# A second FFN whose up products read a scaled and shifted input from the seventh pair on, and wide down products in both mixers

## Chip, cores and metric

One core of a Trainium2 chip runs the whole program in one launch. The metric is the device time of one execution in microseconds (us).

## What is computed

Two transformer blocks after one another, for 256 tokens of width 1024, everything in float32 (x, c, the weights and the result). The first block, cut to what matters:

```
def modulate(x, w, shift, scale):
    return rms_norm(x, w) * (1 + scale[:, None, :]) + shift[:, None, :]

def swiglu(h, w13, w2):
    gu = jnp.einsum('bsd,df->bsf', h, w13)
    g, u = jnp.split(gu, 2, axis=-1)
    return jnp.einsum('bsf,fd->bsd', jax.nn.silu(g) * u, w2)
...
    mod = (c_act @ w_ada + b_ada).reshape(b, 3, 3, D_MODEL)
    x = x + 0.5 * mod[:, 0, 2] * swiglu(modulate(x, norm_w[0], mod[:, 0, 0], mod[:, 0, 1]), ffn_w13[0], ffn_w2[0])
    x = x + mod[:, 1, 2] * hybrid_mixer(modulate(x, norm_w[1], mod[:, 1, 0], mod[:, 1, 1]), ...)
    x = x + 0.5 * mod[:, 2, 2] * swiglu(modulate(x, norm_w[2], mod[:, 2, 0], mod[:, 2, 1]), ffn_w13[1], ffn_w2[1])
```

The FFN width is 2816 (22 blocks of 128). The second block has a mixer of two attentions with gates and an output product, an FFN of width 4096 with squared relu, and a gated embedding; then a last norm.

## The kernel before

**Split products.** Each float32 operand is split into two fp32r parts, a high one that ScalarE writes and a low one that VectorE makes by subtracting the high part. A product is hi x hi + hi x lo + lo x hi. x lies with features on partitions (`m.x[:, k, :]`, k = 0..7, 256 tokens). A *tile* is one 128 x 128 block of weights against all tokens. `tile` (L516) makes it with three matmuls of 256 columns (258 where two shift columns ride along). `wide_tile` (L521) makes it with two: the high weights against both parts of the tokens at once (512 columns, the second 256 of them into the other half of the bank), then the low weights against the high part (256 columns). Whoever reads the bank then has to add its halves.

**Weights.** They come in units of 16 tiles (128 x 2048 float32, 1 MB) through a raw ring of four slots, loaded by SP (`load`, L1384); the load of a unit waits until the unit four before it has been split. ScalarE writes the high half of a unit in two instructions (`hi`), VectorE the low half in two (`lo`, L2474), into a split ring of four slots. Among the units are *modulation pairs* (`ada`): VectorE multiplies a raw unit by silu(c) and sums it, two columns of `mod` each. The planner (`Plan`) writes the order of all engines in one list: `need` takes units three ahead of TensorE, `fill` and `went` put the pending low halves and modulation steps between the other steps. Each engine executes its steps in this order.

**The second FFN** (`second_ffn`, L1004). Pair j (0 to 21) is one unit: the gate block j and the up block j, 8 k each, into two banks. The input `m.h` is x times a column of gains, without the token factor and the shift, so that TensorE can start before the norm is known; the shift rides along as columns 256 and 257, and `glu_evac2` (L646) multiplies each bank by the row of token factors `rbc` on VectorE (gate_scaled, up_scaled), takes the shift column out with ScalarE (shifts), applies the silu (gate_silu), multiplies (glu2) and splits the product (hid_hi, hid_lo). The norm of the stage, from x_norm at pair 0 to norm_rows at pair 1, gives `rbc`. After pair 4, `load_tables` brings the tables of the second block's mixer and `axial_tables` works on them, after pair 8 `bias_table` and `bias_store` follow. The temporary buffers `tmp` (six of 128 x 512) are not used in this stage.

**Down products** run over f = 0..7, with the banks' sums added to x by `residual` (L2619), followed by the input of the next stage (`hx_hi`, `hx_lo`) and its squares. In the FFNs f < 6 is wide (`wide`, L133), in the mixers (`down_1`, `down_2`) every tile has three matmuls.

## Time and profile before

| | |
|---|---|
| median of 3 runs | 1012.15 us (1011.41 to 1012.33) |
| the profiled execution, its own time | 1011.21 us |
| its span in the profile | 1009.4 us |
| PE (matmuls) busy | 982.6 us, 97% |
| PEld (weight loads) busy | 917.6 us, 91% |
| DVE (VectorE) busy | 774.3 us, 77% |
| ACT (ScalarE) busy | 535.0 us, 53% |
| DMA, mean | 212 GB/s |
| up products of the second FFN | 380.5 to 509.8 us of the span |

Times in views are microseconds from the span's start; ns are marked. "idle before <-X" tells what ended the time in which an engine had nothing to do. Weight loads (PEld) overlap matmuls. In a timeline a row merges instructions of one form that follow each other; "[1.37 <-ACT sb_zb L192]" is idle time before the row and what ended it.

### The profile page before, as it was taken

What the parts mean: (1) busy time and instruction counts of PE and PEld (TensorE: products, weight loads), DVE (VectorE), ACT (ScalarE), POOL (GpSimd) and SP (SyncE); (2) the same over time, 40 slices, a digit from 0 to 9 for tenths busy, and PEclk for the clock granted to TensorE, in tenths of its full rate; (3) what the DMA queues carried; (4) which work ended last, traced back from release to release, by engine and by line L of the source; (5) the groups of instructions that cost most, each with busy time, mean ns of one, the idle gap of its engine ahead of it and who ended that gap; (6) DMA issues with size and microseconds to landing.
All of it is one profiled execution on the core that took longest, in us unless ns stands there. A gap on an engine that the chain in (4) does not pass through costs nothing.

```text
span 1009.4 us, 17305 instructions
## 1 busy us (share of the span) xinstructions
PE 982.6 (97%) x7016; PEld 917.6 (91%) x7016; DVE 774.3 (77%) x1420; ACT 535.0 (53%) x927; POOL 11.8 (1%) x32
## 2 busy tenths in 40 slices
PE   5999999999899999999999999999999999999996
PEld 4999998998898999999998988789999988988895
DVE  6999999879976787685776588556778776677665
ACT  5454554437566555353655545664555555455453
POOL 0000000004000000000000000000000000000000
PEclk9999999999999999999999999999999999999998
DMA  9997999865572664678665535364445555545431
GB/s 336 351 344 272 344 343 340 303 212 210 200 253 99 218 213 181 219 239 224 244 227 184 192 126 209 125 183 136 157 173 178 188 188 189 208 168 181 174 106 42
DMA packets 33677, 213.92 MB, mean 212 GB/s; under 512 B 3773, under 2 KB 6717, under 8 KB 8894
## 3 DMA queue, kind: packets, MB, share of 16 engines
q1 hardware_dynamic: 33310, 211.78, 59.5%
q8 instruction: 55, 0.90, 0.3%
q10 hardware_dynamic: 288, 1.05, 0.3%
q14 instruction: 24, 0.20, 0.1%
HBM read 210.19 MB, written 2.62 MB: 211 GB/s over the span
## 4 chain that ended last, share of the span: by engine, by line
PE 80%; DVE 9%; ACT 4%; DMA 4%; issue 2%; SPq 0%; DVEq 0%; ACTq 0%
PE bank L216 78%; DMA sb_raw<-wts 3%; DVE sb_ring L195 2%; ACT sb_ring L192 2%; PE bank L219 2%; ACT sb_tmp L192 1%; DVE sb_junk L204 1%; DVE sb_tq L195 1%; DVE sb_tmp L195 1%; DMA R<-rows 1%; DVE sb_tmp L201 1%; ACT R L192 0%; DMA sb_x<-xt 0%; DVE R_512r L195 0%; DVE sb_tmp L198 0%
## 5 line engine op out<-in xcount | busy, mean ns | idle before, releaser
L216 PE MATMUL bank<-sb_h,sb_ring 128*128 128x258 f32 (+2 forms) x3776 | 496.0, 292 | 4.1 <-DVE sb_h L201 3.9
L216 PEld LDWEIGHTS bank<-sb_h,sb_ring 128*128 128x128 f32 x3776 | 475.5, 190 | 17.8 <-issue 5.9
L195 DVE TENSOR_TENSOR sb_ring<-sb_raw,sb_ring 128x1024 fp32r<-128x1024 f32 (+1 forms) x324 | 385.6, 1205 | 10.4 <-ACT sb_ring L192 10.3
L192 ACT ACTIVATE sb_ring<-sb_raw 128x1024 fp32r<-128x1024 f32 (+1 forms) x324 | 320.4, 1037 | 80.3 <-DMA sb_raw<-wts 47.5
L216 PE MATMUL bank<-R_512r,sb_ring 128*128 128x256 f32 (+1 forms) x1608 | 225.7, 301 | 0.0
L216 PEld LDWEIGHTS bank<-R_512r,sb_ring 128*128 128x128 f32 x1608 | 211.4, 188 | 12.0 <-issue 0.5
L216 PE MATMUL bank<-sb_ring,sb_h 128*128 128x512 f32 (+1 forms) x504 | 112.5, 378 | 0.0
L216 PEld LDWEIGHTS bank<-sb_ring,sb_h 128*128 128x128 f32 x504 | 87.4, 188 | 16.6
L204 DVE CUSTOM_DVE_ANT_0 sb_junk<-sb_raw,sb_csil,sb_cols 128x1024 bf16<-128x1024 f32 x72 | 92.3, 1282 | 1.8
L216 PE MATMUL bank<-R_1024r,sb_ring 128*128 128x512 f32 (+1 forms) x576 | 91.6, 320 | 0.0
L216 PEld LDWEIGHTS bank<-R_1024r,sb_ring 128*128 128x128 f32 x576 | 82.0, 188 | 8.2
L195 DVE TENSOR_TENSOR sb_tq<-bank,sb_rbc 128x256 f32<-128x256 f32 x87 | 33.9, 420 | 50.8 <-ACT sb_zb L192 25.5
L192 ACT ACTIVATE R_512r<-sb_tq 128x256 fp32r<-128x256 f32 x60 | 25.1, 418 | 76.5 <-DVE sb_tq L195 49.7
L192 ACT ACTIVATE sb_tmp<-bank 128x256 f32<-128x256 f32 (+2 forms) x62 | 27.9, 462 | 30.4 <-PE bank L216 27.8
L192 ACT ACTIVATE sb_tmp<-sb_tmp,sb_smx 128x256 f32<-128x256 f32 (+2 forms) x40 | 20.9, 524 | 35.5 <-DVE sb_smx L204 25.3
L201 DVE SCALAR_TENSOR_TENSOR sb_x<-bank,sb_gcol,sb_x 128x256 f32<-128x256 f32 x36 | 17.4, 482 | 27.8 <-PE bank L216 27.4
L192 ACT ACTIVATE sb_h<-sb_x,sb_cols 128x256 fp32r<-128x256 f32 x24 | 14.2, 591 | 37.5 <-DVE sb_x L201 24.0
L195 DVE TENSOR_TENSOR R_512r<-sb_tq,R_512r 128x256 fp32r<-128x256 f32 x60 | 25.2, 420 | 3.9 <-ACT R_512r L192 3.9
L192 ACT ACTIVATE sb_tq<-bank 128x256 f32<-128x256 f32 (+1 forms) x35 | 12.8, 366 | 27.0 <-PE bank L216 27.0
L195 DVE TENSOR_TENSOR sb_tmp<-bank,sb_tmp 128x256 f32<-128x256 f32 x32 | 12.4, 425 | 19.1 <-ACT sb_tmp L192 19.1
L192 ACT ACTIVATE sb_tq<-sb_tq,sb_zb 128x256 f32<-128x256 f32 x26 | 13.3, 510 | 24.3 <-DVE sb_tq L195 24.1
L219 PE MATMUL bank<-sb_con,sb_tmp 128*128 128x128 f32 (+1 forms) x134 | 21.1, 275 | 2.5 <-ACT sb_tmp L192 1.9
(158 smaller groups left out, 555.8 us busy)
## 6 DMA issues: line engine op xcount, KB each, us to landing
...
```

The lines of the kernel that those rows point to most:

```text
L192: return Issued(self.e and self.e.activation(o, i, func, **kw))
L195: return Issued(self.e and self.e.tensor_tensor(*a))
L201: return Issued(self.e and self.e.scalar_tensor_tensor(*a))
L204: return Issued(self.e and self.e.tensor_tensor_reduce(*a))
L216: return Issued(self.e and self.e.matmul(o, w, m, start=start, stop=stop, skip_group_check=True))
L219: return Issued(self.e and self.e.transpose(o, i, ident))
```

## The change

- `second_ffn` has a second way for pairs 6 to 21. The input, scaled by gain and token factor and shifted (the true `modulate`), is made once into eight tiles with a high and a low part (`scaled_tile`: xr_2 on VectorE, scaled_hi on ScalarE, scaled_lo on VectorE). Tiles 0 and 1 come after the evacuation of pair 2, 2 and 3 after pair 3, 4 and 5 after pair 4, 6 and 7 after pair 5. The first six lie in `tmp`, the last two in the region of the tables' one-hot rows, behind `bias_table`.
- Pairs 6 to 21 are products with `wide_tile` (`up_scaled_2`), and `glu_evac_scaled` adds the halves of the banks: up_half (ScalarE copies the second half), up_added (VectorE), silu_added, glu_added, then hid_hi and hid_lo as before.
- `load_tables` moves from pair 4 to after pair 0, `axial_tables` to after pair 2, `bias_table` and `bias_store` from pair 8 to after pair 3.
- In `down_1` and `down_2` the tiles of f < 6 are wide; `residual` and `residual_2` add the second half of the bank in an instruction of their own, and the one that adds the first half waits for it.

```diff
+SCALED_FROM = 6
...
+    def scaled_tile(self, k, b):
+
+        t = self.m.tq.take()
+        self.add("xr_2", k, t)
+        self.fill()
+        self.add("scaled_hi", k, t, b)
+        self.add("scaled_lo", k, t, b)
+        done(t, ("scaled", k))
+
+    def glu_evac_scaled(self, j, banks):
+
+        s, q = self.m.tq.take(), self.m.tq.take()
+        for i, a in enumerate((s, q)):
+            self.add("up_half", j, i, banks[i], a)
+        for i, a in enumerate((s, q)):
+            self.add("up_added", j, i, banks[i], a)
+            done(banks[i], ("up_added", j, i))
+        self.add("silu_added", j, s)
+        self.fill()
+        self.add("glu_added", j, s, q)
+        done(s, ("glu", "f2", j))
+        self.add("hid_hi", "f2", j, q)
+        self.fill()
+        self.add("hid_lo", "f2", j, q)
+        done(q, ("hid", "f2", j))
...
         first = self.glu2("f2", bk, 0, begin)
-        for j in range(1, NH1):
+        self.add("load_tables")
+        scaled = []
+        for j in range(1, SCALED_FROM):
             banks = self.glu2("f2", bk, j, finish if j == 1 else None)
             if j == 1:
                 self.glu_evac2("f2", first, 0)
             self.glu_evac2("f2", banks, j)
-            if j == 4:
-                self.add("load_tables")
+            for k in range(2 * (j - SCALED_FROM + 4), 2 * (j - SCALED_FROM + 5)):
+                if k >= 0:
+                    scaled.append(m.tmp.take() if k < 6 else None)
+                    self.scaled_tile(k, scaled[k])
+            if j == 2:
                 self.add("axial_tables")
-            if j == 8:
+            if j == 3:
                 b = m.banks[7].take()
                 self.add("bias_table", b)
                 done(b, ("bias_table",))
                 self.add("bias_store")
+        for j in range(SCALED_FROM, NH1):
+            banks = [bk.take(), bk.take()]
+            for k in range(8):
+                for i, b in enumerate(banks):
+                    self.mm(128, "up_scaled_2", j, k, i, b, scaled[k])
+            self.glu_evac_scaled(j, banks)
...
+    def up_scaled_2(self, j, k, i, bank, x):
+        e = self.e
+        if k == 0:
+            self.turn(bank)
+        e.wait_ge(*self.at("scaled", k))
+        self.wide_tile(bank.ap, self.m.scaled(k, x), k == 0, k == 7, *([("up", "f2", j)] if k == 7 and i == 1 else []))
...
+    def xr_2(self, k, t):
+        m, e = self.m, self.e
+        self.turn(t)
+        e.wait_ge(*self.at("rbc", "f2"))
+        e.scalar_tensor_tensor(t.ap, m.x[:, k, :], m.acol[:, 16 + k:17 + k], m.rbc, ALU.mult, ALU.mult).then_inc(
+            *self.up("xr", ("xr_2", k)))
+
+    def scaled_lo(self, k, t, b):
+        m, e = self.m, self.e
+        hi, lo = (m.scaled(k, b)[:, i, :] for i in range(2))
+        e.wait_ge(*self.at("scaled_hi", k))
+        e.scalar_tensor_tensor(lo, t.ap, m.mod[:, 48 + k:49 + k], hi.bitcast(F32), ALU.add, ALU.subtract).then_inc(
+            *self.up("scaled_lo", ("scaled", k)))
...
-        if wide(f) and st != "m1":
+        if wide(f):
```

How the instructions stand now, at three places. In these rows of VectorE `sb_ring<-sb_raw` is a low weight half, `ISA sb_junk,sb_mod` with `ISA sb_mod` a modulation step, `sb_tq<-sb_x,sb_acol,sb_rbc` xr_2 and `parts` a scaled tile's low part.

VectorE, before the change, from hid_lo of pair 2 to hid_lo of pair 3:

```order
L195 TENSOR_TENSOR R_512r<-sb_tq,R_512r 128x256
L204 ISA sb_junk,sb_mod<-sb_raw,sb_csil,sb_cols 128x1024
L204 ISA sb_mod 128x1
L204 ISA sb_junk,sb_mod<-sb_raw,sb_csil,sb_cols 128x1024
L204 ISA sb_mod 128x1
L195 TENSOR_TENSOR sb_tq<-bank,sb_rbc 128x256 x2
L195 TENSOR_TENSOR sb_ring<-sb_raw,sb_ring 128x1024
L201 SCALAR_TENSOR_TENSOR sb_tq<-sb_tq,sb_zb 128x256
L195 TENSOR_TENSOR sb_ring<-sb_raw,sb_ring 128x1024
L195 TENSOR_TENSOR R_512r<-sb_tq,R_512r 128x256
```

VectorE, with the change, from hid_lo of pair 2 to the first step of pair 3's evacuation:

```order
L197 TENSOR_TENSOR R_512r<-sb_tq,R_512r 128x256
L203 SCALAR_TENSOR_TENSOR sb_tq<-sb_x,sb_acol,sb_rbc 128x256
L203 SCALAR_TENSOR_TENSOR parts_50<-sb_tq,sb_mod,parts_50 128x256
L203 SCALAR_TENSOR_TENSOR sb_tq<-sb_x,sb_acol,sb_rbc 128x256
L203 SCALAR_TENSOR_TENSOR parts_51<-sb_tq,sb_mod,parts_51 128x256
L200 TENSOR_SCALAR sb_bhalf<-sb_cols 128x16
L197 TENSOR_TENSOR R_256_144<-R_256_57,R_256_59 128x256
L197 TENSOR_TENSOR R_256_145<-R_256_58,R_256_59 128x4x32 x2
L197 TENSOR_TENSOR R_256_146<-R_256_57,R_256_59 128x256
L197 TENSOR_TENSOR R_256_147<-R_256_58,R_256_59 128x4x32 x2
L206 ISA sb_junk,sb_mod<-sb_raw,sb_csil,sb_cols 128x1024
```

Two scaled tiles and the axial tables, which stood behind pair 4, are now ahead of the modulation pair and of pair 3's evacuation.

VectorE, with the change, from the second weight half in pair 5's evacuation to the modulation pair that comes before pair 6's evacuation; the two tiles here are the last that pair 6 reads:

```order
L197 TENSOR_TENSOR sb_ring<-sb_raw,sb_ring 128x1024
L197 TENSOR_TENSOR R_512r<-sb_tq,R_512r 128x256
L203 SCALAR_TENSOR_TENSOR sb_tq<-sb_x,sb_acol,sb_rbc 128x256
L203 SCALAR_TENSOR_TENSOR R_512r<-sb_tq,sb_mod,R_512r 128x256
L203 SCALAR_TENSOR_TENSOR sb_tq<-sb_x,sb_acol,sb_rbc 128x256
L203 SCALAR_TENSOR_TENSOR R_512r<-sb_tq,sb_mod,R_512r 128x256
L206 ISA sb_junk,sb_mod<-sb_raw,sb_csil,sb_cols 128x1024
```

Before the change nothing but the evacuation stood here.

TensorE, with the change, where the bias table stands and pair 6 begins (96 matmuls are pairs 4 and 5; the first two k of pair 6 are shown):

```order
L218 MATMUL bank<-R_1024_60,R_128_61 128x512
L218 MATMUL bank<-sb_h,sb_ring 128x258 x96
L218 MATMUL bank<-parts_50,sb_ring 128x512
L218 MATMUL bank<-parts_50,sb_ring 128x256
L218 MATMUL bank<-parts_50,sb_ring 128x512
L218 MATMUL bank<-parts_50,sb_ring 128x256
L218 MATMUL bank<-parts_51,sb_ring 128x512
```

Before, 366 matmuls of 258 columns stood between the norm's rows and the bias table and 624 after it; each pair of 48 matmuls is now one of 32 from pair 6 on.

## Rows read from the trace of the kernel before

**Rows 1.** The page: busy time of each engine, and TensorE's granted clock in 40 slices

```profile
PE 982.6 (97%) x7016; PEld 917.6 (91%) x7016; DVE 774.3 (77%) x1420; ACT 535.0 (53%) x927; POOL 11.8 (1%) x32
...
PEclk9999999999999999999999999999999999999998
```

**Rows 2.** The page: the chain that ended last, by line

```profile
PE bank L216 78%; DMA sb_raw<-wts 3%; DVE sb_ring L195 2%; ACT sb_ring L192 2%; PE bank L219 2%; ACT sb_tmp L192 1%; DVE sb_junk L204 1%; DVE sb_tq L195 1%; DVE sb_tmp L195 1%; DMA R<-rows 1%; DVE sb_tmp L201 1%; ACT R L192 0%; DMA sb_x<-xt 0%; DVE R_512r L195 0%; DVE sb_tmp L198 0%
```

**Rows 3.** Timeline of ACT, shift columns of pairs 2 and 4: start, length, instruction, [idle before]

```profile
399.40 0.24 ACT L192 ACTIVATE sb_zb<-bank 128x1 f32<-128x1 f32 x2 [0.50 <-PE bank L216]
...
410.89 0.23 ACT L192 ACTIVATE sb_zb<-bank 128x1 f32<-128x1 f32 x2 [0.16 <-PE bank L216]
```

**Rows 4.** Timeline of DVE, residuals in the down product of the second FFN

```profile
540.88 1.00 DVE L201 SCALAR_TENSOR_TENSOR sb_x<-bank,sb_gcol,sb_x 128x256 f32<-128x256 f32 x2 [1.25 <-PE bank L216]
...
548.60 1.00 DVE L201 SCALAR_TENSOR_TENSOR sb_x<-bank,sb_gcol,sb_x 128x256 f32<-128x256 f32 x2 [3.54 <-PE bank L216]
...
564.16 0.48 DVE L201 SCALAR_TENSOR_TENSOR sb_x<-bank,sb_gcol,sb_x 128x256 f32<-128x256 f32 x1 [2.51 <-PE bank L216]
...
571.99 0.48 DVE L201 SCALAR_TENSOR_TENSOR sb_x<-bank,sb_gcol,sb_x 128x256 f32<-128x256 f32 x1 [3.25 <-PE bank L216]
```

**Rows 5.** Timeline of DVE, pair 2 evacuated, a modulation pair, pair 3 begun

```profile
399.91 0.75 DVE L195 TENSOR_TENSOR sb_tq<-bank,sb_rbc 128x256 f32<-128x256 f32 x2
400.58 1.22 DVE L195 TENSOR_TENSOR sb_ring<-sb_raw,sb_ring 128x1024 fp32r<-128x1024 f32 x1
401.71 0.48 DVE L201 SCALAR_TENSOR_TENSOR sb_tq<-sb_tq,sb_zb 128x256 f32<-128x256 f32 x1
402.11 1.22 DVE L195 TENSOR_TENSOR sb_ring<-sb_raw,sb_ring 128x1024 fp32r<-128x1024 f32 x1
...
403.58 1.28 DVE L204 CUSTOM_DVE_ANT_0 sb_junk<-sb_raw,sb_csil,sb_cols 128x1024 bf16<-128x1024 f32 x1
...
406.11 0.75 DVE L195 TENSOR_TENSOR sb_tq<-bank,sb_rbc 128x256 f32<-128x256 f32 x2
```

**Rows 6.** Timeline of DVE, bias column, axial tables, and the bias table's step

```profile
422.60 1.57 DVE L195 TENSOR_TENSOR R<-R,R 128x256 f32<-128x256 f32 x6 [7.53 <-DMA R<-rows]
...
443.65 0.67 DVE L195 TENSOR_TENSOR R<-bank,R 12x512 f32<-12x512 f32 x1
```

**Rows 7.** Timelines: a scaled input step of the first FFN, a split of the second

```profile
15.80 0.48 DVE L201 SCALAR_TENSOR_TENSOR R<-sb_x,sb_acol,sb_rbc 128x256 f32<-128x256 f32 x1 [0.15 <-DVE sb_acol L201]
...
16.32 0.51 ACT L192 ACTIVATE sb_h<-R,sb_mod 128x256 fp32r<-128x256 f32 x1 [1.90 <-DVE R L201]
...
396.58 0.42 ACT L192 ACTIVATE R_512r<-sb_tq 128x256 fp32r<-128x256 f32 x1 [0.63 <-DVE sb_tq L201]
...
397.04 0.42 DVE L195 TENSOR_TENSOR R_512r<-sb_tq,R_512r 128x256 fp32r<-128x256 f32 x1 [0.48 <-ACT R_512r L192]
```

**Rows 8.** Timelines: DVE in mixer 1's down product, and PE at its end

```profile
362.82 0.48 DVE L201 SCALAR_TENSOR_TENSOR sb_x<-bank,sb_gcol,sb_x 128x256 f32<-128x256 f32 x1 [1.36 <-PE bank L216]
...
377.73 0.17 DVE L195 TENSOR_TENSOR sb_h<-sb_mod,sb_h 128x16 fp32r<-128x16 f32 x1
...
380.74 0.48 DVE L201 SCALAR_TENSOR_TENSOR sb_x<-bank,sb_gcol,sb_x 128x256 f32<-128x256 f32 x1 [0.22 <-PE bank L216]
...
380.54 3.75 PE L216 MATMUL bank<-sb_h,sb_ring 128*128 128x258 f32 x30
```

**Rows 9.** Timeline of DVE, last residual of mixer 2's down product

```profile
790.59 0.60 DVE L201 SCALAR_TENSOR_TENSOR sb_x<-bank,sb_x 128x256 f32<-128x256 f32 x1
```

**Rows 10.** Windows and timeline of PE behind its wait in mixer 1

```profile
276.40:279.80 3.40, 3.32 (x16) 3.29 (x17) 3.40 (x7) 1.80 (x7) 0.00 (x0) 0.50 0.98 369
279.80:283.20 3.40, 3.40 (x30) 3.35 (x30) 3.36 (x5) 2.83 (x5) 0.00 (x0) 1.00 0.74 231
...
276.48 1.09 PE L219 MATMUL bank<-sb_con,R 128*96 128x128 f32 x4 [2.96 <-ACT R L192]
277.22 2.84 PE L216 MATMUL bank<-sb_h,sb_ring 128*128 128x258 f32 x12
```

More of the change, by code:

```diff
@@ L304, in __init__ @@
         self.zb = Ring([Buf(sb(f"zb{i}", [128, 2])[:, :]) for i in range(6)])
-        self.tmp = Ring([Buf(sb(f"tmp{i}", [128, 512])[:, :]) for i in range(6)])
+        tmp, self.parts = [], []
+        for i in range(6):
+            tmp.append(Buf(sb(f"tmp{i}", [128, 512])[:, :]))
+            self.parts.append(nc.alloc_sbuf_tensor_at(f"parts{i}", [128, 512], F32R, offset=nc.sbuf_base - 2048)[:, :])
+        self.tmp = Ring(tmp)
         self.tq = Ring([Buf(sb(f"tq{i}", [128, T])[:, :]) for i in range(4)])
@@ L351, in hk2, with scaled @@
         return self.h[:, 0, k, :], self.h[:, 1, k, :]
+    def scaled(self, k, b):
+        a = self.parts[self.tmp.bufs.index(b.buf)] if b else self.reg(46 + 2 * (k - 6), 2 * T, F32R)
+        return a.rearrange("p (s n) -> p s n", s=2)
     def half(self, w, p):
@@ L1030, in second_ffn @@
                 self.add("bias_store")
+        for j in range(SCALED_FROM, NH1):
[4 more added lines that the diff above has]
+            self.glu_evac_scaled(j, banks)
+        for b in scaled[:6]:
+            done(b, ("up", "f2", NH1 - 1))
         self.add("gcol", 2, 0.5)
@@ L1592, in down_1 @@
         e.wait_ge(*self.at("merged_lo", k))
-        self.tile(bank.ap[:, 0:T], self.m.pair(8 + 2 * k), k == 0, k == n - 1,
-                  *([("down", st, f)] if k == n - 1 else []))
+        events = [("down", st, f)] if k == n - 1 else []
+        if wide(f):
+            self.wide_tile(bank.ap, self.m.pair_both(8 + 2 * k), k == 0, k == n - 1, *events)
+        else:
+            self.tile(bank.ap[:, 0:T], self.m.pair(8 + 2 * k), k == 0, k == n - 1, *events)
     def down_2(self, st, f, k, n, bank):
@@ L1600, in down_2 @@
         e.wait_ge(*self.at("sum_lo_2", k))
-        self.tile(bank.ap[:, 0:T], self.m.pair(2 * k), k == 0, k == n - 1, *([("down", st, f)] if k == n - 1 else []))
+        events = [("down", st, f)] if k == n - 1 else []
+        if wide(f):
+            self.wide_tile(bank.ap, self.m.pair_both(2 * k), k == 0, k == n - 1, *events)
+        else:
+            self.tile(bank.ap[:, 0:T], self.m.pair(2 * k), k == 0, k == n - 1, *events)
     def down_3(self, half, f, k, n, bank):
@@ L2027, in silu, with scaled_hi, up_half, silu_added @@
         e.activation(s.ap, bank.ap[:, 0:T], FN.Silu).then_inc(*self.up("silu", ("silu", st, j)))
+    def scaled_hi(self, k, t, b):
+        m, e = self.m, self.e
+        if b:
+            self.turn(b)
+        else:
+            e.wait_ge(*self.at("bias_table"))
+        e.wait_ge(*self.at("xr_2", k))
+        e.activation(m.scaled(k, b)[:, 0, :], t.ap, FN.Identity, bias=m.mod[:, 48 + k:49 + k]).then_inc(
+            *self.up("scaled_hi", ("scaled_hi", k)))
+    def up_half(self, j, i, bank, a):
+        e = self.e
+        self.turn(a)
+        e.wait_ge(*self.at("up", "f2", j))
+        e.activation(a.ap, bank.ap[:, T:2 * T]).then_inc(*self.up("up_half", ("up_half", j, i)))
+    def silu_added(self, j, s):
+        e = self.e
+        e.wait_ge(*self.at("up_added", j, 0))
+        e.activation(s.ap, s.ap, FN.Silu).then_inc(*self.up("silu", ("silu", "f2", j)))
     def hid_hi(self, st, j, q):
@@ L2623, in residual @@
         e.wait_ge(*self.at("down", st, f))
-        if wide(f) and st != "m1":
+        if wide(f):
             e.scalar_tensor_tensor(m.x[:, f, :], bank.ap[:, T:2 * T], m.gcol[:, i:i + 1], m.x[:, f, :], ALU.mult,
@@ L3054, in residual_2 @@
         e.wait_ge(*self.at("down", "m2", f))
+        if wide(f):
+            e.scalar_tensor_tensor(x, classes(bank.ap[:, T:2 * T]), 0.5, x, ALU.mult, ALU.add).then_inc(
+                *self.up("vector_own"))
+            e.wait_ge(*self.last())
         e.scalar_tensor_tensor(x, classes(bank.ap[:, 0:T]), 0.5, x, ALU.mult, ALU.add).then_inc(
```

16 lines of the change are left out of this document (13 added, 3 removed).

## Prediction

> **What bounds the kernel now.** I read the page first: its busy shares, the granted clock in slices and the chain that ended last. PE is busy for 97% of the span, and 78% of the chain are its matmuls on L216; the clock is full in nearly every slice [rows 1, 2]. So a microsecond leaves the kernel only if TensorE has less to issue, and a microsecond comes in wherever TensorE has to wait. VectorE, at 77%, is the engine that could make it wait: it makes the low half of every weight unit. The timelines of the stages that the change touches say how near it is.
>
> In the up products of the second FFN, ScalarE's two shift columns wait for TensorE at the end of every pair, at 399.40 for pair 2 and at 410.89 for pair 4: 5.745 us a pair of 16 tiles, 359.1 ns a tile of three matmuls with 258 columns [rows 3]. In the down products of the same FFN a wide chunk of 22 tiles takes 7.72 us, 350.9 ns a tile of one matmul with 512 and one with 256 columns, and a narrow chunk 7.83 us, 355.9 ns a tile [rows 4].
>
> **What TensorE saves.** Pairs 6 to 21 hold 16 x 16 = 256 tiles; at 359.1 - 350.9 = 8.2 ns each that is 2.1 us. The down product of mixer 1 now takes (380.74 - 362.82)/50 = 358.4 ns a tile (the first f is out after 14 of 64 tiles, the last after all) [rows 8]; 48 wide tiles save 7.5 ns each, 0.36 us. For mixer 2 I take the narrow 355.9 ns, so 48 x 5.0 = 0.24 us. Together 2.7 us, and no more, though a third of these matmuls goes: the streamed columns stay nearly the same, 768 for 774.
>
> The Trainium skill (TensorE: Matmul & The Clock Gate, "Wait — 56ns, not 53.3ns?") has a matmul cost its columns at 2.4 GHz and 2.5 ns. An estimate from that page is 330 ns for the narrow tile and 325 for the wide one, 5 ns saved and 1.3 us in the FFN where the rows give 2.1; the trace has both tiles longer, so the sum goes by the trace.
>
> **What VectorE gets.** Before pair 6 may run, eight scaled tiles must be ready, two after the evacuation of each of pairs 2 to 5. In VectorE's queue each is xr_2, then scaled_lo, and between them the engine stands still for ScalarE's scaled_hi: the order puts nothing there, since no piece of weights is pending. The same three steps are in the first FFN: VectorE starts at 15.80, ScalarE at 16.32 and is busy 0.51; VectorE follows a ScalarE step after some 0.03 (396.58 + 0.42 to 397.04) [rows 7]. With 0.40 for scaled_lo until the next can start (401.71 to 402.11 [rows 5]) a tile holds the queue for 0.52 + 0.51 + 0.03 + 0.40 = 1.46 us, eight of them for 11.7. Bounds: 0.80 a tile if all waiting were hidden, 6.4 in all.
>
> I follow VectorE from the evacuation of pair 2, which starts at 399.91 and now is behind by 0.5 us already because of the modulation pair ahead of it. In order come, by rows 5 and 6:
> - four evacuations with their two weight halves, 403.58 - 399.91 = 3.67 each: 14.7
> - one modulation pair, 406.11 - 403.58: 2.5
> - eight scaled tiles: 11.7
> - the axial tables, 1.57, and a step of one short row ahead of them: 1.7
> - the bias table's one step, 0.67 at 443.65: 0.6
> - ScalarE now splits a unit right ahead of the silu of pair 5, and glu2 may wait for it; no row shows this order, I put 0.5 between 0 and 1: 0.5
>
> Sum 31.7 us, to 431.6. All of this now happens under cover of TensorE; the tables and the bias step, now behind pairs 4 and 8, come into the same stretch. The 7.53 us in which VectorE waits for the gains' DMA [rows 6] are room for some tiles, and the sum uses it: nothing in it is idle time but the waits for ScalarE. That wait goes because load_tables moves seven weight loads ahead on SP's queue. Its five DMAs then stand ahead of a weight load; the ring runs three units ahead of TensorE, and I cost this at nothing, hidden by those units (without them it could cost as much as the wait for these tables does now, 7.5 us).
>
> **The stage before.** Mixer 1's down product gets six more residual steps in VectorE's queue, each followed by one that waits for it, 0.52 us each: 3.1 us. The last shift part, which the first tile of pair 0 needs, is there at 377.90, and TensorE arrives at 380.54, now 380.18 [rows 8]; idle time of VectorE between its steps there swallows a part. I take 1.0 us by which pair 0, its norm and so the evacuation of pair 2 start later; the bounds are 0 and 2. In mixer 2 the same six steps make x(7) late by 1 to 2 us; it starts at 790.59 now [rows 9], and TensorE wants its result only in the 15th tile of the next stage, 4.9 us in. I cost that at nothing; without that cover it would be 1 to 2 us.
>
> **The wait.** The eighth tile is then ready at 431.6 + 1.0 + 0.1 = 432.7, and the two matmul tiles that need it end pair 6 at 433.4. Without the change pair 6 ends at 410.89 + 2 x 5.745 - 0.27 = 422.1. So TensorE loses 11.3 us there; what mixer 1 and pair 6 would have saved (0.5 us) vanishes in the wait. After it 240 tiles still save 2.0 us, and mixer 2 saves 0.24. In the evacuations from pair 6 on VectorE has 3.6 us of work in 5.6, ScalarE 0.4 us more than before; both are free again.
>
> **The clock.** TensorE would stand idle twice for 4 to 5 us, before tile 4 of pair 6 (pair 4's evacuation is late) and before tile 6. The trace has one such case: after 2.96 us idle the granted clock in 276.4 to 279.8 is 0.50, the level of 1.2 GHz, and 12 matmuls take 2.84 us, where 12 of the 48 in a pair's 5.745 us [rows 3] are 1.44 [rows 10]. I take one such stretch behind the second wait, 3.4 us at half speed: 1.7 us lost, of which 0.2 falls into a wait. Bounds 0 and 5.6, a whole pair more.
>
> The Trainium skill (TensorE: Matmul & The Clock Gate, "What's actually happening") says the low clock is what an idle TensorE has by default and that only sustained activity lifts it. By that rule pair 6, which runs in pieces, would not lift it; it is the mechanism of rival 3.
>
> **Sum:** + 11.3 + 1.5 - 2.2 = +10.6 us. The profiled execution took 1011.21, the median of three is 1012.15, so 0.9 above it; on the median the forecast is 1022.7, **slower by 1.0%**.
>
> **Rivals.**
> 1. The scaled tiles fit beside TensorE, no wait arises: 1012.15 - 2.7 = 1009.4, faster. For it: VectorE is only 77% busy, and idle for 7.5 us in this stretch [rows 6]. Against it: the tile is needed 4.9 us into pair 6, at about 421.3, so the queue would have to get through in 21.4 us what I add up to 31.7. It decides if an evacuation and two tiles took under 4.1 us instead of 6.6.
> 2. The tiles take nearer to 0.8 us, the waits for ScalarE being shorter, and there is no slip in mixer 1: 11.3 falls to 5.0, one wait is short and the clock loss 0.5: 1012.15 + 5.0 + 0.5 - 2.2 = 1015.5.
> 3. The clock stays at half through pairs 6 and 7: 4 us more than the forecast: 1026.7. For it: two waits in a row. Against it: in rows 10 it was back after 3.4 us, with TensorE busy.
>
> **Chances.** Forecast 0.6, rival 1 0.07, rival 2 (and what lies between) 0.18, rival 3 0.12, and 0.03 for a wait that just eats the gain. The range 1015 to 1026.5 takes in rival 2 and most of rival 3. What this kernel's runs can tell from no change is about 0.2%, 2 us: faster 0.07, within it 0.04, slower 0.89.
>
> **What would show it.** In the timeline of PE after some 416: idle time in pair 6 in front of the matmuls that read parts 4 and 5 and again before R_512r tiles 6 and 7, released by VectorE's scaled_lo; PE's share of the span falls to 96%. VectorE without idle time beyond 0.6 us from 397 to 432. Granted clock 0.5 in a stretch of 3 to 4 us there. Pairs 7 to 21 at 5.61 us each. Wrong would be the forecast if pair 6 had no wait (then the eight tiles cost VectorE less than I say), if TensorE waited for weights in place of tiles, or if pairs 7 to 21 stayed at 5.75 us.

## The result and the profile after

| | before | with the change |
|---|---|---|
| median (4 runs each, on the same chip) | 1011.78 us (1010.47 to 1012.33) | 1023.77 us (1023.39 to 1024.48) |
| ratio to before | | 1.0121 (95% interval 1.0108 to 1.0133) |
| the profiled execution, its own time | 1011.21 us | 1023.77 us |
| its span | 1009.4 us | 1022.0 us |
| first matmul of pair 0 of the second FFN | 380.54 | 380.64 |
| sums of mixer 2's norm on TensorE | 577.34 | 588.51 |
| sums of the MLP's norm on TensorE | 795.65 | 808.03 |

The change makes the kernel slower by 1.2%, 12.0 us. The three marks of the table (first matmul that reads `sb_h`; first that reads `sb_acc` in the next two stages) place the loss in the spans: nothing ahead of the second FFN, 11.1 us between the first and the second mark, 1.2 us more in mixer 2. I use the distance from the first mark to the second below, 196.80 us before and 207.87 after: it leaves out what happens in earlier stages.

The page after, as in [rows 1]: TensorE has 352 matmuls fewer and is busy 1.9 us longer, and the granted clock is down in one slice, the one that has the FFN's pair 6.

```profile
PE 984.5 (96%) x6664; PEld 901.9 (88%) x6664; DVE 786.3 (77%) x1448; ACT 545.2 (53%) x935; POOL 11.8 (1%) x32
...
PEclk9999999999999999799999999999999999999999
```

TensorE's timeline after, pair 6 in the first three rows and pair 7 behind (`parts` are scaled tiles 0 to 5, `R_512r` 6 and 7):

```profile
417.45 2.98 PE L218 MATMUL bank<-parts,sb_ring 128*128 128x512 f32 x16
424.70 3.10 PE L218 MATMUL bank<-parts,sb_ring 128*128 128x512 f32 x8 [4.27 <-DVE parts L203]
433.02 3.11 PE L218 MATMUL bank<-R_512r,sb_ring 128*128 128x512 f32 x8 [5.22 <-DVE R_512r L203]
435.93 4.94 PE L218 MATMUL bank<-parts,sb_ring 128*128 128x512 f32 x24
440.70 1.57 PE L218 MATMUL bank<-R_512r,sb_ring 128*128 128x512 f32 x8
442.11 4.37 PE L218 MATMUL bank<-parts,sb_ring 128*128 128x512 f32 x24
```

Two waits for VectorE's scaled tiles, 4.27 and 5.22 us. The eight matmuls behind each take 3.1 us where eight of pair 7 take 1.57. Windows of the same stretch (TensorE busy first, the granted clock third from the end) say why: half clock from some 423.5, 3 us into the first wait, to 437.2, through the work between the waits, the whole second wait and the work behind it.

```profile
420.00:424.00 4.00, 0.43 (x3) 0.10 (x1) 3.59 (x6) 1.26 (x3) 0.00 (x0) 0.94 0.71 81
424.00:428.00 4.00, 3.10 (x8) 2.09 (x8) 1.67 (x4) 2.65 (x6) 0.00 (x0) 0.50 0.86 139
428.00:432.00 4.00, 0.00 (x0) 0.00 (x0) 3.85 (x7) 0.99 (x3) 0.00 (x0) 0.50 0.70 78
432.00:436.00 4.00, 2.98 (x9) 2.38 (x10) 2.90 (x6) 2.85 (x4) 0.00 (x0) 0.50 0.87 141
436.00:440.00 4.00, 4.00 (x21) 3.46 (x21) 4.00 (x7) 1.50 (x4) 0.00 (x0) 0.85 0.75 86
```

VectorE's timeline after: a scaled tile (xr_2, scaled_lo, and the next xr_2), the axial tables, the starts of the evacuations of pairs 4 and 5, and the last scaled_lo.

```profile
404.18 0.48 DVE L203 SCALAR_TENSOR_TENSOR sb_tq<-sb_x,sb_acol,sb_rbc 128x256 f32<-128x256 f32 x1
405.23 0.48 DVE L203 SCALAR_TENSOR_TENSOR parts<-sb_tq,sb_mod,parts 128x256 fp32r<-128x256 f32 x1 [0.58 <-ACT parts L194]
405.64 0.48 DVE L203 SCALAR_TENSOR_TENSOR sb_tq<-sb_x,sb_acol,sb_rbc 128x256 f32<-128x256 f32 x1
...
407.17 1.56 DVE L197 TENSOR_TENSOR R<-R,R 128x256 f32<-128x256 f32 x6
...
419.44 0.76 DVE L197 TENSOR_TENSOR sb_tq<-bank,sb_rbc 128x256 f32<-128x256 f32 x2 [1.00 <-ACT sb_zb L194]
...
427.70 0.75 DVE L197 TENSOR_TENSOR sb_tq<-bank,sb_rbc 128x256 f32<-128x256 f32 x2 [1.59 <-ACT sb_zb L194]
...
433.94 0.48 DVE L203 SCALAR_TENSOR_TENSOR R_512r<-sb_tq,sb_mod,R_512r 128x256 fp32r<-128x256 f32 x1 [0.58 <-ACT R_512r L194]
```

A tile takes 405.64 - 404.18 = 1.46 us of the queue, and the axial tables no longer wait ([rows 6]: 7.53). New are the two waits for the shift columns, 1.00 and 1.59 us. ScalarE's timeline has their reason, the split of the next unit right ahead of them; its last two rows are up_half of two late pairs, 5.62 us apart ([rows 3]: 5.745).

```profile
425.49 1.99 ACT L194 ACTIVATE sb_ring<-sb_raw 128x1024 fp32r<-128x1024 f32 x2
427.38 0.21 ACT L194 ACTIVATE sb_zb<-bank 128x1 f32<-128x1 f32 x2
...
504.10 0.66 ACT L194 ACTIVATE sb_tq<-bank 128x256 f32<-128x256 f32 x2 [0.63 <-PE bank L218]
...
509.72 0.66 ACT L194 ACTIVATE sb_tq<-bank 128x256 f32<-128x256 f32 x2 [0.63 <-PE bank L218]
```

In mixer 2, the last low part of the MLP's input (VectorE) and the start of the MLP (TensorE) before the change:

```profile
791.77 0.48 DVE L201 SCALAR_TENSOR_TENSOR sb_h<-sb_x,sb_cols,sb_h 128x256 fp32r<-128x256 f32 x1 [0.58 <-ACT sb_h L192]
...
790.01 5.80 PE L216 MATMUL bank<-sb_h,sb_ring 128*128 128x512 f32 x32
```

With the change, VectorE's last residual and that low part, and TensorE at the start of the MLP:

```profile
805.49 0.62 DVE L203 SCALAR_TENSOR_TENSOR sb_x<-bank,sb_x 128x256 f32<-128x256 f32 x1
806.69 0.49 DVE L203 SCALAR_TENSOR_TENSOR sb_h<-sb_x,sb_cols,sb_h 128x256 fp32r<-128x256 f32 x1 [0.58 <-ACT sb_h L194]
```

```profile
800.99 5.47 PE L218 MATMUL bank<-sb_h,sb_ring 128*128 128x512 f32 x28
807.23 0.96 PE L218 MATMUL bank<-sb_h,sb_ring 128*128 128x512 f32 x4 [0.77 <-DVE sb_h L203]
```

The residual starts 14.9 us later than in [rows 9], while TensorE came into mixer 2 only 11.2 us later: VectorE lost 3.7 us within the stage. Before, the low part was there at 792.25 and TensorE came to it after 28 of the 32 matmuls, at some 795.0 (an estimate from the row): 2.7 us of cover. The 3.7 us are 1.0 more than that, and TensorE stands and waits.

### The profile page after: what moved, and what is told of

Same layout as the page of the kernel before. It is cut to its first block, busy times and chain, and to the rows that moved or that the text cites. A ratio compares the mean times of both kernels' runs of the same rounds, so it can differ in the third digit from the quotient of the medians.

```text
span 1022.0 us, 16605 instructions
## 1 busy us (share of the span) xinstructions
PE 984.5 (96%) x6664; PEld 901.9 (88%) x6664; DVE 786.3 (77%) x1448; ACT 545.2 (53%) x935; POOL 11.8 (1%) x32
## 4 chain that ended last, share of the span: by engine, by line
PE 78%; DVE 13%; ACT 5%; issue 3%; DMA 1%; ACTq 0%; DVEq 0%
PE bank L218 76%; DVE sb_ring L197 4%; ACT sb_ring L194 2%; PE bank L221 2%; DVE sb_x L203 1%; ACT sb_tmp L194 1%; DVE sb_junk L206 1%; DVE sb_acc L197 1%; DVE sb_tmp L197 1%; DVE sb_tmp L203 1%; DVE sb_tq L197 1%; DVE sb_tq L203 1%; DVE sb_h L203 0%; ACT R L194 0%; DVE R_512r L197 0%
## 5 line engine op out<-in xcount | busy, mean ns | idle before, releaser
L218 PE MATMUL bank<-sb_h,sb_ring 128*128 128x256 f32 (+2 forms) x3008 | 404.2, 294 | 5.3 <-DVE sb_h L203 4.7
L218 PEld LDWEIGHTS bank<-sb_h,sb_ring 128*128 128x128 f32 x3008 | 383.3, 190 | 19.4 <-issue 6.1
L218 PE MATMUL bank<-R_512r,sb_ring 128*128 128x512 f32 (+1 forms) x1640 | 251.6, 313 | 5.2 <-DVE R_512r L203 5.2
L218 PEld LDWEIGHTS bank<-R_512r,sb_ring 128*128 128x128 f32 x1640 | 227.3, 189 | 25.0 <-DVE R_512r L203 6.0
L218 PE MATMUL bank<-parts,sb_ring 128*128 128x512 f32 (+1 forms) x384 | 72.3, 345 | 4.3 <-DVE parts L203 4.3
L218 PEld LDWEIGHTS bank<-parts,sb_ring 128*128 128x128 f32 x384 | 60.5, 192 | 13.4 <-DVE parts L203 4.9
L197 DVE TENSOR_TENSOR sb_tq<-bank,sb_tq 128x256 f32<-128x256 f32 x44 | 17.2, 421 | 48.8 <-ACT sb_tq L194 48.8
L197 DVE TENSOR_TENSOR sb_tq<-bank,sb_rbc 128x256 f32<-128x256 f32 x55 | 21.8, 420 | 27.8 <-PE bank L218 25.0
L203 DVE SCALAR_TENSOR_TENSOR sb_x<-bank,sb_gcol,sb_x 128x256 f32<-128x256 f32 x42 | 20.2, 482 | 28.7 <-PE bank L218 28.1
L194 ACT ACTIVATE sb_tq<-bank 128x256 f32<-128x256 f32 (+1 forms) x67 | 23.3, 372 | 33.1 <-PE bank L218 33.0
```

The source lines that it names most:

```text
L194: return Issued(self.e and self.e.activation(o, i, func, **kw))
L197: return Issued(self.e and self.e.tensor_tensor(*a))
L203: return Issued(self.e and self.e.scalar_tensor_tensor(*a))
L218: return Issued(self.e and self.e.matmul(o, w, m, start=start, stop=stop, skip_group_check=True))
```

## The experiments

Each kernel ran beside the kernel before on the same chip; ratios are to that. Medians of different experiments come from different chips, on which the kernel before took 1011.38 to 1012.0 us, so two experiments are compared by their ratios or in the trace. Five profiled executions (e1, e2, e3, e7, e9) had the clock at half for 6.8 us instead of 3.4 in mixer 1, which moves everything behind by about 1.2 us; the distance between the two marks is free of that. It has a scatter of its own: e1 and e11 have the FFN of the kernel before and show 196.30 and 196.92, the one without and the other with the small wait for weights at 481 that is discussed under e12; the change, e2 and e3 have one FFN and show 207.87 to 208.36.

| kernel | median, us | ratio (95% interval) | first to second mark, us |
|---|---|---|---|
| before | 1011.78 | | 196.80 |
| the change | 1023.77 | 1.0121 (1.0108 to 1.0133) | 207.87 |
| e1_mixers_only | 1013.14 | 1.0014 (1.0005 to 1.0023) | 196.30 |
| e2_ffn_only | 1022.22 | 1.0105 (1.0091 to 1.0119) | 207.95 |
| e3_mixer2_narrow | 1022.84 | 1.0111 (1.0098 to 1.0125) | 208.36 |
| e4_piped_tiles | 1019.2 | 1.0078 (1.0065 to 1.009) | 204.67 |
| e5_busy_pe | 1021.3 | 1.0099 (1.0085 to 1.0113) | 207.52 |
| e6_tables_late | 1021.66 | 1.0103 (1.0088 to 1.0119) | 207.21 |
| e7_no_wait | 1014.11 | 1.0021 (1.0012 to 1.003) | 198.67 |
| e8_from_ninth | 1011.17 | 1.0001 (0.9992 to 1.001) | 196.37 |
| e9_store_in_four | 1009.0 | 0.9975 (0.9965 to 0.9985) | 194.58 |
| e10_split_behind | 1023.13 | 1.0116 (1.0102 to 1.013) | 208.51 |
| e11_mixer2_three | 1011.11 | 0.9999 (0.9991 to 1.0008) | 196.92 |
| e12_before_store | 1010.62 | 0.9992 (0.9983 to 1.0001) | 196.24 |

### Which part costs what: e1, e2, e3

e1 is the kernel before with wide down products in both mixers; e2 is the change without them; e3 is the change with `down_2` and `residual_2` as before. Of e2's edit the part in `down_1`; `down_2` goes back the same way, and the added steps of `residual` and `residual_2` go (e3 has only `down_2` and `residual_2`):

```diff
-        if wide(f):
-            self.wide_tile(bank.ap, self.m.pair_both(8 + 2 * k), k == 0, k == n - 1, *events)
-        else:
-            self.tile(bank.ap[:, 0:T], self.m.pair(8 + 2 * k), k == 0, k == n - 1, *events)
+        self.tile(bank.ap[:, 0:T], self.m.pair(8 + 2 * k), k == 0, k == n - 1,
+                  *([("down", st, f)] if k == n - 1 else []))
```

> The kernel before with only the wide down products of both mixers. Forecast on record: minus 0.4 us in mixer 1 taken back by a slip, minus 0.24 us in mixer 2, so 1011.2 to 1011.8. Theory from the trace of the change: the six added residual steps make the last x of mixer 2 so late (3.8 us in that trace) that the next stage's TensorE waits for it, plus 1.4 us; mixer 1 plus 0.2 us; so 1013.4. Rival: the mixers cost nothing and the whole 12 us come from the FFN: 1011.8.

> The change without the wide down products of the mixers. Theory: the wait of TensorE in pair 6 remains, 1022.2 (before plus 10.4). TensorE idle for 4 to 5 us ahead of tile 4 and ahead of tile 6 of pair 6. Rival (the mixers' slip makes the wait): below 1015.

> The change with narrow tiles in mixer 2's down product alone. Theory: minus 1.45 us against the change, 1022.3, and no idle time of TensorE at the start of the MLP. Rival (mixer 2 is neutral, as the prediction had it): 1023.8 to 1024.0.

e1 and e2 came out as their theories had it, where the prediction had put the mixers at nothing or a small gain: the FFN costs some 10.5 us, the mixers some 1.4. e3 came out between its theory and its rival, nearer the theory: by the ratios 1.0 us below the change where 1.45 was expected, and the two intervals overlap. The traces are clearer on mixer 2. From the second mark to the third the change and e1, with wide tiles there, take 219.52 and 219.49 us; the kernel before, e2 and e3 take 218.31, 218.29 and 218.31. TensorE's timeline of e1 has the place of the 1.2 us:

```profile
791.05 4.82 PE L218 MATMUL bank<-sb_h,sb_ring 128*128 128x512 f32 x26 [0.15 <-DVE sb_x L203]
796.65 0.97 PE L218 MATMUL bank<-sb_h,sb_ring 128*128 128x512 f32 x4 [0.77 <-DVE sb_h L203]
```

### Is it x(7) that comes late, or the wide tiles themselves: e11

The kernel before with three wide blocks in mixer 2 in place of six:

```diff
-        self.tile(bank.ap[:, 0:T], self.m.pair(2 * k), k == 0, k == n - 1, *([("down", st, f)] if k == n - 1 else []))
+        events = [("down", st, f)] if k == n - 1 else []
+        if f < 3:
+            self.wide_tile(bank.ap, self.m.pair_both(2 * k), k == 0, k == n - 1, *events)
+        else:
+            self.tile(bank.ap[:, 0:T], self.m.pair(2 * k), k == 0, k == n - 1, *events)
```

> The kernel before with only three blocks (f = 0 to 2) of mixer 2's down product wide, and mixer 1 and the FFN as they were. Theory (in e1_mixers_only six more residual steps of 0.65 us each make x(7) 3.7 us late on VectorE, which has no idle time there, and TensorE waits 0.9 us for it and more before it; up to some 2.5 us there is cover): three steps make it 1.9 us late, TensorE does not wait at the start of the MLP, and the 24 wide tiles save 0.1 us: 1011.9 us beside 1012.0, a ratio of 0.9999. Rival (TensorE's loss in e1 comes with the first wide tile, for example from a bank that comes free later): 0.5 us or more slower than before, 1012.5.

```profile
789.90 5.80 PE L218 MATMUL bank<-sb_h,sb_ring 128*128 128x512 f32 x32
```

A ratio of 0.9999 and no wait: the MLP's first 32 matmuls run in one piece, and the second mark is 218.18 us from the third. x(7) starts 1.9 us later than before (792.52 against 790.59), inside the 2.7 us of cover. So the loss of e1 does not come with the first wide tile but once x(7) is later than the cover; e11 halves the wide tiles and the extra steps together, and what tells them apart is e1's wait, which VectorE's low part ends.

### Is it VectorE's queue that sets the end of pair 6: e4, e6, e10

e4 is e2 with the tiles written in pairs, so that VectorE has the second xr_2 while ScalarE does the first scaled_hi:

```diff
+                for i in range(2):
+                    self.add("xr_2", k + i, ts[i])
+                for i in range(2):
+                    self.add("scaled_hi", k + i, ts[i], scaled[k + i])
+                for i in range(2):
+                    self.add("scaled_lo", k + i, ts[i], scaled[k + i])
```

> FFN part of the change alone (e2_ffn_only, 1022.22 us), and each pair of scaled tiles is written as xr, xr, hi, hi, lo, lo, so that VectorE does the second xr_2 while ScalarE does the first scaled_hi. Theory (VectorE's queue sets the end of pair 6, and a tile costs it 1.46 us of which 0.5 is standing still for ScalarE): a pair of tiles takes about 0.48 + 0.48 + 0.54 + 0.42 = 1.9 to 2.1 us instead of 2.9, four pairs save 3 to 4 us, all of it in TensorE's two waits: 1018.2 to 1019.2 us. Rival (TensorE in pair 6 waits for something else too, weights or ScalarE's split of a unit right ahead of the shift columns): under 1 us saved, 1021.5 us or more.

VectorE's timeline of e4 has two tiles in 405.31 - 403.44 = 1.87 us in place of 2.92, and TensorE's has the first wait at 1.75 in place of 4.27:

```profile
403.44 0.87 DVE L204 SCALAR_TENSOR_TENSOR sb_tq<-sb_x,sb_acol,sb_rbc 128x256 f32<-128x256 f32 x2
404.50 0.89 DVE L204 SCALAR_TENSOR_TENSOR parts<-sb_tq,sb_mod,parts 128x256 fp32r<-128x256 f32 x2 [0.19 <-ACT parts L195]
405.31 0.17 DVE L201 TENSOR_SCALAR sb_bhalf<-sb_cols 128x16 f32<-128x16 f32 x1
```

```profile
421.86 1.67 PE L219 MATMUL bank<-parts,sb_ring 128*128 128x512 f32 x8 [1.75 <-DVE parts L204]
...
429.13 2.93 PE L219 MATMUL bank<-R_512r,sb_ring 128*128 128x512 f32 x8 [5.59 <-DVE R_512r L204]
```

By the ratios e4 is 2.7 us faster than e2, in the trace 3.3, where the theory had 3 to 4. From the evacuation of pair 2 to the end of tile 7 VectorE needs 29.7 us (399.77 to 429.47) in place of e2's 33.9; not all of the 4.2 us arrive, since now all eight matmuls behind the second wait run at half clock after it (2.93 us), where in e2 four of them lay in time that was waited. The queue with its waits for ScalarE sets the end of pair 6.

e6 is e2 with tiles 6 and 7 in a region of their own and the table steps late:

```diff
-        self.add("load_tables")
...
-            if j == 2:
-                self.add("axial_tables")
-            if j == 3:
...
+            if j == 8:
+                self.add("load_tables")
+            if j == 12:
...
+        self.add("axial_tables")
```

> FFN part alone (1022.22 us), with tiles 6 and 7 in a region of their own, so that the tables need not come first: load_tables after pair 8, the bias table after pair 12, the axial tables after pair 21. Theory (VectorE's queue ahead of tile 7 sets the end of pair 6): it loses 1.7 us of axial tables and 0.6 us of the bias step, TensorE's waits shrink by 2.3 us; against that the bias table's matmul comes back behind pair 6 (0.86 us, it was in front of it: no change in the sum) and the bias store's DMA, now at a place where no wait covers it, can hold up weight loads as it did in e7_no_wait (2.6 us on TensorE): 1019.9 us without that hold-up, 1022.5 with all of it. Which of the two shows in ScalarE's idle time for DMA in front of its split at 480 to 510 and in TensorE's wait behind it.

In time this is no gain that can be told from noise: the ratio is 1.0103 beside e2's 1.0105. In the trace tile 6's matmuls start 1.6 us earlier behind the first mark (430.91 - 380.61 against 433.76 - 381.88 in e2), not 2.3. VectorE's timeline says where the bias table's 0.6 us went: its wait for the shift columns of pair 4 is 1.60 us now and was 1.00. The step had stood in time that VectorE waits for ScalarE anyway.

```profile
417.38 0.76 DVE L197 TENSOR_TENSOR sb_tq<-bank,sb_rbc 128x256 f32<-128x256 f32 x2 [1.60 <-ACT sb_zb L194]
```

Of the 1.6 us TensorE gives back some 0.9 for the bias table's matmuls, which now stand behind pair 6 and not in front of its waits, and 0.9 behind the bias store, where ScalarE's split waits 10 us for its weights; in return pair 7 has less of the half clock (4.57 us to its last eight matmuls against 5.53 in e2). At the second mark 0.7 is left.

```profile
498.97 2.01 ACT L194 ACTIVATE sb_ring<-sb_raw 128x1024 fp32r<-128x1024 f32 x2 [10.08 <-DMA sb_raw<-wts]
```

e10 is e2 with ScalarE's split moved behind the silu in the evacuations of pairs 3 to 5, against the waits of 1.00 and 1.59 us for the shift columns:

```diff
+            if j in (3, 4, 5):
+                last = max(n for n, s in enumerate(self.steps) if s[0] == "shifts")
+                h = max(n for n in range(last) if self.steps[n][0] == "hi")
+                step = self.steps.pop(h)
+                g = max(n for n, s in enumerate(self.steps) if s[0] == "gate_silu")
+                self.steps.insert(g + 1, step)
```

> FFN part of the change alone (e2_ffn_only, 1022.22 us; from the first matmul of pair 0 to the norm's sums of mixer 2 its trace has 207.95 us), with ScalarE's split of the next unit moved from in front of the shift columns to behind the silu in the evacuations of pairs 3 to 5. Theory (VectorE waits 1.00 and 1.59 us there for the shift columns, since ScalarE does 1.99 us of splitting first, and these 2.6 us are on the chain to tile 7): both waits go, 205.4 us in the trace, 1019.6 us. Rival (VectorE then waits as long for the silu, or for hid_hi, behind the same split): 207.5 us or more, 1021.8 us.

A miss, and on the rival's side. Both waits are gone, and three new ones of 1.25 us stand in their place: the low half that VectorE makes in the evacuation is of the very unit whose split was moved.

```profile
412.71 1.22 DVE L197 TENSOR_TENSOR sb_ring<-sb_raw,sb_ring 128x1024 fp32r<-128x1024 f32 x1 [1.25 <-ACT sb_ring L194]
```

So putting the split behind the shift columns does not remove the waits, it makes them longer (3.75 us in three places, before 2.59 in two). ScalarE is bound to VectorE by the scaled tiles, gets to its 1.99 us of splitting only after the second of them (417.23 in the change), and VectorE needs both results soon after. Whether the split could go ahead of the tiles, where ScalarE waits for VectorE too, was not tried.

### What the clock costs: e5

e2, with matmuls into an unused bank ahead of TensorE's two waits. They add work and compute nothing that is used.

```diff
+        if j == SCALED_FROM and i == 0 and k in (4, 6):
+            e.wait_ge(*self.at("bias_table"))
+            w = self.weights(128)
+            for _ in range(15 if k == 4 else 18):
+                e.matmul(self.m.banks[7].ap.rearrange("p (s n) -> p s n", s=2), w[0], self.m.scaled(0, self.m.first_scaled),
+                         True, True)
```

> FFN part of the change alone (1022.22 us); in pair 6 TensorE issues 15 matmuls of 512 columns into a bank nobody reads ahead of its wait for tile 4, and 18 ahead of its wait for tile 6, some 3.5 and 4.2 us of work inside waits of 4.3 and 5.2 us. They add work and no result. Theory (of the 13.8 us about 0.8 to 1.5 are the clock at half behind the two waits): the granted clock stays at 1.0 in 420 to 436, the four tiles behind the first wait take 1.4 instead of 2.9 us, which only lengthens the second wait, and the last two tiles of pair 6 end 0.7 to 0.8 us earlier: 1021.4 us. If the clock also costs time after pair 6, up to 1020.7. Rival (the half clock lies wholly inside time that is waited anyway): 1022.2 us; rival (clock falls whatever the engine does): 1022.2 and the windows at 0.5 as before.

```profile
424.02 0.98 PE L218 MATMUL bank<-parts,sb_ring 128*128 128x512 f32 x4 [0.39 <-DVE parts L203]
425.48 5.15 PE L218 MATMUL bank<-parts,sb_ring 128*128 128x512 f32 x22 [0.48 <-DVE parts L203]
432.35 0.97 PE L218 MATMUL bank<-R_512r,sb_ring 128*128 128x512 f32 x4 [1.71 <-DVE R_512r L203]
433.81 1.28 PE L218 MATMUL bank<-R_512r,sb_ring 128*128 128x512 f32 x4 [0.48 <-DVE R_512r L203]
```

```profile
424.00:428.00 4.00, 3.50 (x16) 2.72 (x17) 1.82 (x5) 2.98 (x6) 0.00 (x0) 1.00 0.90 137
428.00:432.00 4.00, 2.64 (x12) 1.80 (x10) 3.36 (x6) 0.99 (x3) 0.00 (x0) 1.00 0.76 92
432.00:436.00 4.00, 3.17 (x12) 2.47 (x13) 3.39 (x6) 3.06 (x5) 0.00 (x0) 0.78 0.84 135
```

With TensorE busy in the waits the clock stays at 1.0 to 432, where the change has 0.50. The time does not settle what this is worth: the median is near the expected one, but the intervals of e5 and e2 overlap. The trace moved by 0.4 us where 0.8 was expected. The rows show both why it is little and why it is less than expected. With the clock at full, tile 6's four matmuls end early and the last four wait 0.48 for tile 7, so most of what the half clock took was time that had to be waited. And the clock falls once more at some 434.2, behind the wait of 1.71, for 3.4 us: pair 6 ends 1.07 us behind the start of its last four matmuls, where full clock has 0.7, and pair 7 still takes 5.62 us for its 24. What the kernel would take with the clock at full throughout is not shown.

### A version without the stall: e7, e8, e9, e12

e7 is e4 with e6's placement and wide products from pair 7 on:

```diff
-SCALED_FROM = 6
+SCALED_FROM = 7
```

> Mixers as before; scaled input from pair 7 on; the two tiles behind each of pairs 2 to 5 are written with xr_2 twice, scaled_hi twice, scaled_lo twice, so that VectorE does not stand still; tables and bias table stand behind pairs 8, 12 and 21 (the last two tiles lie where the axial tables come later). Theory: the tiles are ready before TensorE needs them, no wait, 15 pairs save 0.13 us each: 1009.8 (minus 2.0). Rival (wide up products cost TensorE or its banks something of their own): 1011.8 or more.

It missed that by some 4 us. Its timelines (TensorE, then ScalarE) show 3.7 of them, a short wait for tile 6 and one for weights:

```profile
428.68 1.67 PE L219 MATMUL bank<-R_512r,sb_ring 128*128 128x512 f32 x8 [1.13 <-DVE R_512r L204]
...
495.58 4.44 PE L219 MATMUL bank<-parts,sb_ring 128*128 128x512 f32 x24 [2.59 <-DVE sb_ring L198]
```

```profile
491.24 2.01 ACT L195 ACTIVATE sb_ring<-sb_raw 128x1024 fp32r<-128x1024 f32 x2 [11.92 <-DMA sb_raw<-wts]
```

The bias store, 1.5 MB in one DMA, was issued at 465.07. e8 has `SCALED_FROM = 8`, and `load_tables` and the bias table behind pairs 4 and 8 as in the kernel before.

> FFN part alone, no stall intended: like e7_no_wait (tiles in their own region and in interleaved pairs behind pairs 2 to 5, axial tables last), but pairs 8 to 21 are wide instead of 7 to 21, and load_tables and the bias table stand behind pairs 4 and 8 as in the kernel before. Theory (e7 lost 1.1 us to tile 6 and 2.6 us to the weights held up by the late bias store): neither is left, 14 pairs save 0.13 us each, 1.8 us, less up to 0.5 for a hold-up at the store as the kernel before has it: 1010.2 to 1010.7 us, granted clock 0.5 only around 280. Rival (the wide form itself is worth nothing once it runs free, because VectorE and ScalarE then trail): 1012 us or more.

A miss: no faster than before (1.0001), where 1010.2 to 1010.7 us was expected. No tile is waited for now, but weights behind the store (issued at 444.74) still are:

```profile
475.22 4.45 PE L219 MATMUL bank<-parts,sb_ring 128*128 128x512 f32 x24 [1.20 <-DVE sb_ring L198]
...
481.36 4.45 PE L219 MATMUL bank<-parts,sb_ring 128*128 128x512 f32 x24 [0.29 <-DVE sb_ring L198]
```

e9 is e8 with the store in four DMAs, one behind each of pairs 8 to 11:

```diff
-                self.add("bias_store")
+            if 8 <= j < 12:
+                self.add("bias_store", j - 8)
...
-        dst = m.scratch[:, :].rearrange("h (m w) -> h m w", m=64)[:, :, 0:512]
+        dst = m.scratch[:, :].rearrange("h (m w) -> h m w", m=64)[:, 16 * q:16 * q + 16, 0:512]
```

> As e8_from_ninth (1011.17 us), but the bias store of 1.5 MB, which stood as one DMA behind the bias table, is four DMAs of a quarter each behind pairs 8 to 11, with weight loads between them. Theory (in e8 the wide pairs save 1.8 us and give 1.5 back in two waits for weights, 1.20 us at 475.22 and 0.29 at 481.36, because the one store holds up the weight loads by more than the ring's three units cover): ScalarE's idle time for DMA in front of its splits is under 4 us at each part, TensorE has no wait in 440 to 500, and from the first matmul of pair 0 to the norm's sums of mixer 2 the trace has 195.0 us (e8 196.4, before 196.8): 1009.6 to 1010.0 us. Rival (the wait is not the store's but the wide pairs' own, whose units are wanted sooner than the loads bring them): the waits stay, 1011.2 us.

Windows of e8, and the same of e9: in e9 TensorE is busy throughout, and neither its waits nor ScalarE's for the DMA are left in 440 to 500.

```profile
474.00:481.00 7.00, 5.80 (x33) 4.91 (x32) 6.96 (x11) 3.35 (x7) 0.00 (x0) 1.00 0.82 287
481.00:488.00 7.00, 6.71 (x39) 5.84 (x39) 5.71 (x10) 4.82 (x9) 0.00 (x0) 1.00 0.77 288
```

```profile
474.00:481.00 7.00, 7.00 (x41) 6.14 (x41) 5.33 (x9) 5.21 (x9) 0.00 (x0) 1.00 0.81 311
481.00:488.00 7.00, 7.00 (x42) 6.13 (x41) 4.97 (x9) 4.73 (x10) 0.00 (x0) 1.00 0.65 228
```

e9 beats both kernels: 2.5 us faster than before (ratio 0.9975, 0.9965 to 0.9985). e12 asks how much of that the store alone gives, with every product as before.

> The kernel before with nothing changed but the bias store, which is four DMAs of a quarter behind pairs 8 to 11, as in e9_store_in_four (ratio 0.9975; 194.6 us in the trace from the first matmul of pair 0 to the norm's sums of mixer 2, before 196.8). It tells how much of e9's 2.2 us is the store and how much are the 14 wide pairs. Theory (the store costs the kernel before only what its trace shows, TensorE's wait of 0.19 us at 480.94 and at most 0.2 of unnamed gaps, and 1.8 us are the wide pairs): 196.4 to 196.6 us in the trace, 1011.2 us, ratio 0.9996. Rival (the store is most of the gain, wide pairs are worth little): 195.5 us or less, ratio 0.9987 or below.

196.24 us in the trace, 0.56 less than before, and TensorE's wait of 0.19 us at 480.94 is gone, as is the wait of ScalarE's split that the kernel before has:

```profile
470.48 2.01 ACT L192 ACTIVATE sb_ring<-sb_raw 128x1024 fp32r<-128x1024 f32 x2 [8.31 <-DMA sb_raw<-wts]
```

The time lies between theory and rival. The ratio's interval (0.9983 to 1.0001) reaches no change, and e1 has 196.30 without TensorE's wait though its store is the old one; so up to some 0.5 us is what the single store costs the kernel before in an execution where it shows, and no run settles its mean. Beside e12, where no such wait is left either, the 14 wide pairs of e9 give 196.24 - 194.58 = 1.66 us, 0.119 a pair, 7.4 ns a tile; the ratios (0.9992 and 0.9975) say 1.7 us too.

## Why the prediction was right, point by point

The forecast was 1022.7 us and slower; it came out at 1023.77, inside the range. The mechanism was the forecast's: TensorE waits twice in pair 6, for tiles 4 and 6, released by VectorE's scaled_lo, and the clock falls to half. Two of its own signs failed: VectorE has idle time of 1.00 and 1.59 us where none above 0.6 was to be, and the half clock lasts 13.7 us, not 3 to 4. That the number is off by only 1 us is in part luck: two terms were too small and two were left out, and they partly cancel. The terms:

- **TensorE saves 8.2 ns a tile.** Pairs 7 to 21 come 5.62 us apart against a predicted 5.61, and e9 against e12 gives 7.4 ns.
- **A scaled tile takes 1.46 us of VectorE's queue.** Exactly that. What it is made of was right too: e4 took most of the standing still out, and 3.3 us came back in the trace.
- **VectorE's chain of 31.7 us.** It was 434.4 - 400.5 = 33.9. The term that was mis-sized is the wait for ScalarE, put at 0.5 between 0 and 1 for the silu of pair 5: it measured 1.00 + 1.59, ahead of it, at the shift columns of pairs 4 and 5. e10's reordering only moved it, and longer. The rest fits within 0.2. The 0.6 for the bias table stands in the sum but is no cost of its own: the step fills part of the first of these waits, which is 1.60 without it (e6).
- **The slip of 1.0 us from mixer 1.** It was 0.6 (evacuation of pair 2 at 400.51, before 399.91).
- **The 0.36 us that mixer 1's wide tiles save** did not appear at all: pair 0 starts 0.10 later. Its shift part is written from 380.37 to 380.54, before from 377.73, and TensorE starts at 380.64 after 0.44 us of idle time; e1 and e3 have the same 0.44, e2, without the wide tiles, has none. The prediction let it vanish in the later wait, with the same sum.
- **Weights.** The tables' five DMAs, seven weight loads earlier on the queue, were hidden as predicted: TensorE had no wait for weights.
- **Clock, 1.5 us net of one stretch of 3.4 us.** The stretch was some 13.7 us, from within the first wait to behind the second, four times as long. The cost was near the forecast all the same, and that is luck: by the rows 0.8 us in the last four matmuls of pair 6 (tile 7 is ready at 434.42, pair 6 ends at 435.93, at full clock 0.7 us behind the tile) and 0.6 in pair 7 (4.94 against 4.37). e5 says why a longer stretch costs little more: it lies in time that is waited anyway. In e2, with the same FFN, pair 7 lost 1.3 us to the half clock and not 0.6, so the cost differs between executions. The granted clock is 0.50 in the windows around the eight matmuls between the waits. By the Trainium skill's rule that only sustained activity lifts the clock (TensorE: Matmul & The Clock Gate, "What's actually happening"), these eight would not do it, and the rows agree. It did not go as far as rival 3, a second pair at half.
- **Mixer 2, costed at nothing.** This step failed. Six steps of 0.65 us (0.52 in mixer 1) made x(7) 3.7 us late, not 1 to 2: the only idle time of VectorE between them is its wait for ScalarE's high half of the same input (0.58 us and once 1.24, before 0.58 and 1.22), and that does not shrink. The cover of 2.7 us did not reach: TensorE waits 0.77 us at 807.23, and its 28 matmuls before that take 0.4 longer. The stage costs 1.2 us in the trace and e1's ratio says 1.4 for the mixers. e11, with three of the steps, costs nothing.
- **Left out:** the bias table on TensorE, 0.9 us, stood behind pair 8 and now stands ahead of pair 6, so that it is in the 13.8 us of the next paragraph and not lost at the second mark. The store's hold-up, up to 0.56 us, is hidden in the stall after the change.

The account to the second mark: 435.93 - 422.1 = 13.8 at the end of pair 6, 0.6 of the clock in pair 7, less 0.9 for the bias table, which before comes later, less 15 x 0.125 = 1.9 in the wide pairs, less 0.56 for the store: 11.0, where the marks say 577.34 to 588.51, 11.2. The forecast had +10.6 for the whole; the later eighth tile (+1.7) and mixer 2 (1.2 against -0.2) added to that, the bias table and the store took 1.4 off; the spans say +12.6, the medians +12.0.

Rival 1 was wrong for this kernel, but its price for the FFN was right, as e9 shows: without waits 14 wide pairs give 1.7 us, where 8.2 ns a tile makes 1.8. Its 0.6 us for the mixers did not appear.
